# Storing a table in parts between other blocks, and a new order of the last loads and stores of a stage, in a one-core diffusion step

## The reference, cut to what matters

```
def peer(h, p):
    q = jnp.einsum('nd,dq->nq', x, p['w_query']).reshape(n, PK_HEADS, 2, HALF_KEY)
    s1 = jnp.einsum('nhc,hkc->nhk', q[:, :, 0], p['sub_keys'][0])
    s2 = jnp.einsum('nhc,hkc->nhk', q[:, :, 1], p['sub_keys'][1])
    ...
    gates = jax.nn.softmax(top_s.astype(F32), axis=-1).astype(h.dtype)
    ...
        act = jax.nn.gelu(jnp.einsum('nd,nhkd->nhk', xb, eu[ib]))
        return jnp.einsum('nhk,nhkd->nd', act * gb, ev[ib])
```

## Time and profile before

| | |
|---|---|
| median of three runs | 2981.67 us |
| the profiled execution, its own time | 2970.88 us |
| its span, first to last instruction | 2969.1 us |
| mean granted TensorE clock | 0.981 |
| PE busy | 2821.5 us (95%) |
| VectorE busy | 2174.8 us (73%) |
| ScalarE busy | 1228.4 us (41%) |
| moved by DMA | 815.60 MB, mean 275 GB/s |

### The profile page before, as it was taken

The page is one execution under the profiler, slowest core; times in us unless marked ns, Lnnn a source line. Parts: engine busy times, 40 slices in busy tenths (PEclk is TensorE's granted clock), DMA queues, the critical chain, the costliest instruction groups (busy, mean ns, idle before and its releaser), DMA issues.

```text
span 2969.1 us, 59639 instructions
## 1 busy us (share of the span) xinstructions
PE 2821.5 (95%) x24170; PEld 2480.4 (84%) x24170; DVE 2174.8 (73%) x3115; ACT 1228.4 (41%) x1895; POOL 846.7 (29%) x586
## 2 busy tenths in 40 slices
PE   7899999899999999989999999999999999999998
PEld 5799999577877769889998888888887877877776
DVE  2455532666656653479989999988888998999988
ACT  3333333333333333353346666654443433433433
POOL 0000000122222220038894444431123342233432
PEclk9999999799999989999999999999999999999999
DMA  9533332234333433256569999999999999999997
GB/s 404 236 126 127 127 127 93 108 123 147 134 119 141 171 117 113 85 190 221 213 239 360 371 401 395 392 401 411 417 407 412 418 417 418 417 418 418 417 418 316
DMA packets 207690, 815.60 MB, mean 275 GB/s; under 512 B 81520, under 2 KB 101104, under 8 KB 118416
## 3 DMA queue, kind: packets, MB, share of 16 engines
q1 hardware_dynamic: 104320, 527.05, 46.0%
q0 software_dynamic: 36864, 268.45, 21.7%
q10 hardware_dynamic: 66320, 17.43, 2.6%
HBM read 772.50 MB, written 40.37 MB: 274 GB/s over the span
## 4 chain that ended last, share of the span: by engine, by line
PE 29%; DMA 12%; DVE 9%; issue 4%; POOL 1%; ACT 1%; SPq 0%; DVEq 0%; ACTq 0%
DMA work<-act_table 11%; PE ps L1884 10%; PE ps L1885 5%; DVE work L2533 2%; DVE x L2422 2%; PE ps L2273 2%; PE ps L2274 2%; PE ps L2275 2%; DVE wlo L1851 1%; DVE wlo L2538 1%; PE ps L2168 1%; PE ps L2170 1%; PE ps L2169 1%; PE ps L1876 1%; PE ps L1878 1%
## 5 line engine op out<-in xcount | busy, mean ns | idle before, releaser
L1884 PE MATMUL ps<-hboth,whi 128*128 128x512 f32 x1664 | 588.8, 398 | 12.2 <-DVE wlo L1851 12.2
L1885 PE MATMUL ps<-hboth,wlo 128*128 128x256 f32 x1664 | 463.5, 279 | 0.0
L2273 PE MATMUL ps<-whi,hboth 128*128 128x512 f32 x1024 | 403.2, 394 | 24.4 <-DVE wlo L2538 20.2
L2274 PE MATMUL ps<-wlo,hboth 128*128 128x512 f32 x1024 | 400.8, 391 | 0.0
L2275 PE MATMUL ps<-whi,hboth 128*128 128x512 f32 x1024 | 400.6, 391 | 0.0
L2312 POOL DMA_INDIRECT work<-expert_v,idx x128 | 263.4, 2058 | 460.4 <-DVE work L2533 444.7
L1884 PEld LDWEIGHTS ps<-hboth,whi 128*128 128x128 f32 x1664 | 312.3, 188 | 85.4 <-DVE wlo L1851 14.5
L2312 POOL DMA_INDIRECT x<-u_rows,idx x128 | 235.4, 1839 | 432.0 <-DVE x L2422 248.7
L1885 PEld LDWEIGHTS ps<-hboth,wlo 128*128 128x128 f32 x1664 | 313.4, 188 | 0.0
L2533 DVE SCALAR_TENSOR_TENSOR work<-work,dots 128x2048 f32<-128x2048 f32 x127 | 297.7, 2344 | 0.1
L265 PE MATMUL ps<-hhi,whi 128*128 128x384 f32 x768 | 256.6, 334 | 1.9 <-DVE wlo L254 1.9
(11 more groups left out here) (380 smaller groups left out, 6220.3 us busy)
## 6 DMA issues: line engine op xcount, KB each, us to landing
raw<-expert_u SPq DMA_DIRECT2D x85, 1024.0 KB
x<-w_ada SPq DMA_DIRECT2D x64, 1024.0 KB, 5.3
work<-expert_v SPq DMA_DIRECT2D x64, 1024.0 KB
raw<-expert_v SPq DMA_DIRECT2D x64, 1024.0 KB
raw<-w_in SPq DMA_DIRECT2D x50, 1024.0 KB, 4.8
raw_more<-expert_u SPq DMA_DIRECT2D x43, 1024.0 KB
z<-w_ada SPq DMA_DIRECT2D x32, 1024.0 KB, 13.7
raw<-w_out SPq DMA_DIRECT2D x16, 1024.0 KB, 4.8
```

The source lines that it names most:

```text
L1884: pe.matmul(both, whi[:, r, k, :], hboth[:, :, k, CTX:T], start=(k == 0), stop=False)
L1885: last = pe.matmul(both[:, 0], wlo[:, r, k, :], hhi[:, k, CTX:T], start=False, stop=(k == KD - 1))
L2273: pe.matmul(bank, ah, vh[:, part], start=first, stop=False)
L2274: done = pe.matmul(bank, ah, vl[:, part], start=False, stop=False)
```

## The change

The table's sets are stored in parts by keys. Sets 0, 1 and 2 go in eight parts of 16 keys each, one behind each of the first eight blocks of the next set. Set 3 goes in 16 parts of 8 keys, one behind every second block of rest, from the first to the thirty-first. ScalarE's loop of rest is written out, since the parts differ. SP's order after its loop becomes: wait for all table stores, expert_v block 0, spill 123, first read of the tables, load of block 143, spill 124, expert_v block 1, second read, expert_v blocks 2 and 3 with spills 125 and 126 behind them, spill 127. ScalarE issues no spills.

```
         SETS = LAT // GT
         UPS_PER_SET = USCAT // SETS
+        SET_PARTS = 8
+        PART = NK // SET_PARTS
+        LATE = 8
...
+        SET_0 = 16 * SET_PARTS * 2
+        SET_1 = 16 * (SET_PARTS + NK // LATE)
...
                 with sp.Fori(0, TURNS) as it:
                     rest(it)
-                load_fixed(M_DOWN - 1)
+                sp.wait_ge(stage_out[0].sem, SET_0)
+                sp.wait_ge(stage_out[1].sem, SET_1)
+                load_v(expert_v[0], 0)
+                spill(NK - 5)
                 for r in range(2):
-                    sp.wait_ge(stage_out[r].sem, 16 * (SETS // 2))
                     sp.wait_ge(spilled[r].sem, 16 * 2)
                 groups(0, 0)
-                load_v(expert_v[0], 0)
+                load_fixed(M_DOWN - 1)
+                spill(NK - 4)
                 load_v(expert_v[1], 1)
                 groups(1, 2)
                 for r in range(2):
                     assert raw_at(M_DOWN - 3 + r) == r
                     sp.wait_ge(w_low[1 - r].sem, (M_DOWN - 3 + r) // 2 + 1)
                     load_v(expert_v[2 + r], 2 + r)
+                    spill(NK - 3 + r)
+                spill(NK - 1)
                 for r in range(2):
                     sp.wait_ge(spilled[r].sem, 16 * (NK // 2))
...
                     if q % 16 == 0 and s >= 2:
-                        act.wait_ge(stage_out[s % 2].sem, 16 * (s // 2))
+                        act.wait_ge(stage_out[s % 2].sem, 16 * SET_PARTS * (s // 2))
...
-                def store_set(s):
+                def store_keys(s, key, n):
                     act.wait_ge(staged.sem, GT // 4 * (s + 1))
-                    act.dma_start(gate_table[:, 0:NK, s * GT:(s + 1) * GT], stage[:, s % 2]).then_inc(stage_out[s % 2].sem, 16)
+                    act.dma_start(gate_table[:, key:key + n, s * GT:(s + 1) * GT], stage[:, s % 2, key:key + n]
+                                  ).then_inc(stage_out[s % 2].sem, 16)
...
                     m, g, q = M_SCAT + 2 * i, U_SCAT + 2 * i, QUADS * i
+                    s_done, i_set = i // (SCAT // SETS) - 1, i % (SCAT // SETS)
+                    store = s_done >= 0 and 2 * i_set < SET_PARTS
...
                     gelu_sum(g)
+                    if store:
+                        store_keys(s_done, PART * (2 * i_set), PART)
...
                     gelu_sum(g + 1)
-                    if (q + QUADS) % (GT // 4) == 0:
-                        store_set(q // (GT // 4))
+                    if store:
+                        store_keys(s_done, PART * (2 * i_set + 1), PART)
...
-                with act.Fori(0, TURNS) as it:
-                    for n in range(TURN_OF):
-                        rest(it, n)
-                def spill_own(g):
-                    act.wait_ge(u_out.sem, g + 1)
-                    act.dma_start(act_table[:, g, :], act_f[:, g % 2]).then_inc(spilled[g % 2].sem, 16)
-
-                spill_own(NK - 5)
+                for n in range(TURNS * TURN_OF):
+                    rest(n // TURN_OF, n % TURN_OF)
+                    if n % 2 == 0 and n // 2 < NK // LATE:
+                        store_keys(SETS - 1, LATE * (n // 2), LATE)
                 for n in range(REST - TURNS * TURN_OF):
                     rest(TURNS, n)
-                    spill_own(NK - 4 + n)
...
-                pool.wait_ge(stage_out[0].sem, 16 * (SETS // 2))
-                pool.wait_ge(stage_out[1].sem, 16 * (SETS // 2))
+                pool.wait_ge(stage_out[0].sem, SET_0)
+                pool.wait_ge(stage_out[1].sem, SET_1)
```

## The result

The changed kernel took 3013.53 us, the median of four runs (3009.72 to 3016.79), against 2983.88 us for four runs of the kernel before (2972.07 to 2986.54). The medians differ by 29.7 us; the recorded ratio is 1.0117, interval 1.0084 to 1.015. So the kernel is **slower by about 1%**, clear of noise, above the forecast range (its top was 3010) and past the bound of 0.5%. The profiled execution's span is 3012.3 us, 43.2 us over the one before.

The account below looks back on a forecast made before the run. The prediction took DMA transfers to bound the down loop, with PE busy 95% of the span; terms 0 + 0.5 - 1.3 + 2.8 + 4.0 = +6.0 us on 2981.67 gave 2987.7 us, range 2972 to 3010.

Parts of the forecast that it names:

- Do parts wait for each other at issue?: ScalarE's part stores: no issue is held behind an earlier part, taken as 0, the other end kept as a rival.
- The rival built on it: ScalarE held at its part issues until the part before is out: 20 to 57 us slower, 3002 to 3039, chance 0.12.
- the packet rule of the Trainium skill: DMA queues: read as giving q10 over nine packets for one, against the trace's 331 to 287.
- The bound of the down loop: Down loop: ends when the DMA engines have moved its bytes, at 418 GB/s and 5.66 us a block.
- More issues on ScalarE at no cost: ScalarE's sequencer: 31 more issues of 0.38 us, 12 us, covered by idle time before each eviction, so 0.
- Buffer reuse: Refilling the half a set leaves: later parts could delay copies, between 0 and 1 us net, twice; taken as 0.5.
- When set 3 lands: Last table store, in rest: lands at 2202 to 2206, the same time as before; SP's restart 1.3 us sooner.
- rival 1: Table store off the path, SP doesn't wait: at most 10.9 us gained, time 2971 to 2979, chance 0.20.
- Load 143 and the restart: End of rest: load 143 and a spill behind SP's wait, +2.8; late load 143 then empties the DMA engines, +4.
- -1.3 + 2.8 + 4.0: Restart terms: SP's sooner restart, load and spill moved behind the wait, and empty DMA engines after late load 143.
- Rival 3: Blocked restart is worse, store landing at 2212 or later, load 143's lateness full on PE: +12 to +22, chance 0.18.

Follow-up runs that it names:

- The probe: The kernel before, with three 1 KB stores issued by ScalarE, each one block after the whole store of sets 0, 1 and 2; 3048.76 us in one execution.
- scatter_spread: The kernel before with sets 0 to 2 stored in smaller parts over 15 blocks of the next set, 45 issues; 3015.98 against 2976.95 us, ratio 1.0113.
- parts_by_sp: The kernel before with all table parts and the last spills issued by SP, load 143 ahead of the wait; 2995.0 against 2971.5 us, ratio 1.0071.
- late_parts: The kernel before with only set 3 stored in 16 parts of 8 keys in rest; 2983.17 against 2976.95 us, ratio 1.0036.
- thin_parts: The kernel before with 24 part issues for sets 0 to 2, each of 256 packets, plus an early 17 MB copy; 3010.25 us, scatter 428.7 us.
- sp_order: The kernel before, whole stores kept, with SP's new order after its loop and the last five spills by SP; 2976.68 against 2976.95 us, ratio 1.0004.

## Why the prediction was wrong

**The step that failed is "Do parts wait for each other at issue?"**, which I took at 0. Its lower bound rested on SP's eight issues, none held. They are loads of 8 KB rows and small reads, 128 or 256 packets each. They say nothing of an issue behind thousands of short rows, and there was one row that did: the spill behind the store's tail, 3.74 us. I set that one aside since the program's start shows a jump as long. The probe shows what it was a small case of: 28 to 30 us where the whole store is ahead. The nearest row was the one of the same queue and the same kind of work, not the many of another kind. The rival built on it (20 to 57 us, chance 0.12) held the result: the medians differ by 29.7, and scatter by 37.0. In its place the runs show ScalarE standing still for 78.3 us behind its own issues, PE idle for 26.4 us more in scatter and, what no term of the forecast had, PE busy for 10.6 us more with the clock at its lower level for part of the time.

The rival's own arithmetic was not right either. It had each part held for the time that it drains beside the traffic (12.1 us against 6.5), and from that a threshold: parts that drain in under 9.4 us would be free. scatter_spread was made for it and failed. Its 2.9 us of idle time was read over 16 scatter blocks and 35 of rest; the scatter stage alone has 159.0/64 = 2.5. The traces show how much the rows ahead matter, if one counts q10's packets asked for and moved. Of ScalarE's 223 issues from 1600 us on, in all profiles but parts_by_sp, all 31 with 1733 or more packets ahead took 0.97 us or longer; of the 142 with fewer than 345 ahead, all but three took under 0.5. Between the two it goes both ways: 1002 ahead went through in 0.38 us, 709 ahead took 11.1. Nor is the queue always empty when a held issue goes out: the changed kernel's part at 1961.35 left after 6.07 us with 1820 still ahead. What decides in the middle, and what lets go, was not found. Rows were never told apart from bytes on ScalarE's queue; that SP's eight issues carry megabytes in few rows and are not held speaks for rows.

The Trainium skill (DMA: Bandwidth & Descriptors, Anatomy of one DMA) says, of GpSimd's path, that one can emit many descriptors before their generation shows. For one transfer on ScalarE's queue the rows here are alike, 16384 rows for 0.38 us of issue. Of the next transfer on the same queue that sentence says nothing, and there the probe has 28 us.

The forecast also read the packet rule of the Trainium skill (DMA: Bandwidth & Descriptors, Queues, rings and completion order) wrongly, as nine for one in favour of q10. The rule lets an engine drain a packet of descriptors from each ring in turn, SP's ring too, so two queues that both have rows waiting come out near one for one; the 331 to 287 do not speak against it.

The other points:

- **The bound of the down loop: right, as far as it was tried.** All profiles have 746 to 756 us behind the last eviction, whatever SP waited for, and the page's slices there stand at 417 or 418 GB/s before and after. A restart 10.7 us earlier against the end of rest, in late_parts, gave 3.5 us.
- **More issues on ScalarE at no cost: right** in itself. thin_parts has its 24 for nothing.
- **Buffer reuse, 0.5 us: too small in kind.** For the changed kernel no such wait shows. For whole stores it can be 10 to 15 us in an execution, since the landing of a whole store (97 us in one case, 124 in another) straddles the 107.8 us.
- **When set 3 lands: the wait stayed, the rate was wrong.** I gave q10 331 packets a block, as the kernel before; in the changed one it moved 10225 over 2110 to 2217, or 531 in 5.56 us:

```profile
q10 hardware_dynamic: 10225, 2.58, 10.7%
```

  The parts ask for 512 rows a block, so it moved what it was asked. Yet the last 489 packets, after 2217, took until 2240, and SP's first transfer behind them went out 203 us after the first eviction of rest, against 204 before. "The same time as before" came true by luck, with the rate wrong. SP's wait was 6.2 us, under the 9 to 14 forecast, and in late_parts it was gone: rival 1's event, with at most 3.5 us of rival 1's gain and 15.6 us of holds against it.
- **Load 143 and the restart: the lateness came, its price is open.** The last two steps of rest take 6.4 us more in the changed kernel and 6.6 in sp_order, and what follows is 5 us shorter in both, in one profile each, so about +1.5 against a sum of -1.3 + 2.8 + 4.0 = +5.5. The median of sp_order cannot tell either from 0. ScalarE's wait for load 143 was 4.6 us and not 10, since the copy itself stood 5.7 us later in rest than before.
- **Rival 3** (12 to 22 us at the restart) did not come as told. Rest did cost 12.1 us, but only 6.4 of them at its end; the other 5.7 hold two held issues of 5.9 and 6.8 us.

## What to carry to other kernels

A store of many short rows should be the last thing that its queue's engine issues for as long as it drains: the issue itself is cheap, and the *next* one on that engine pays. Cutting such a store into parts makes every part a next one. An engine with nothing to issue behind it and nothing urgent to compute would be the place for it; no run here tried that. And when a wait is removed from an engine that feeds a loop bound by transfers, expect little: here 10.7 us of an earlier restart were worth 3.5.

## What was not expected of the hardware

- An issue of 1 KB was held 28 to 30 us behind 16384 rows of 256 bytes on the same queue, and let go when nearly all of them had passed; loads on SP's queue were held up to 6 us behind parts of 1024 and 2048 rows.
- While ScalarE was held, q10 moved the rows of a 4 MB store in 30 us. Beside the scatter stage's transfers such a store takes 97 to 124 us, and beside rest 207 to 209.
- Not every issue behind undrained rows is held. In scatter_spread 13 waits of ScalarE for its copies come from 45 parts. Few rows ahead pass, many do not; the line between was not settled.
- In rest the same queue moved 331 packets a block as one store and 531 as parts. Why parts get more was not tried.
- TensorE's granted clock fell to 0.50 for 6.8 us in a gap of 5.7 us in PE's work, made by a hold, and for some 31 us in the whole scatter stage. A stall of another engine costs PE more than the time that it waits.
